# Stick-breaking attention: value products with the values stationary for pairs of heads, and their normalisation transposed

## The reference, cut to what matters

```python
def stick_breaking(q, k, v, qpos, kpos):
    z = jnp.einsum('bqhd,bkhd->bhqk', q, k).astype(jnp.float32) * (B_DIM ** -0.5)
    before = kpos[None, :] < qpos[:, None]
    log_keep = jnp.where(before, jax.nn.log_sigmoid(-z), 0.0)
    rev = lax.cumsum(log_keep, axis=3, reverse=True)
    after = jnp.concatenate([rev[..., 1:], jnp.zeros_like(rev[..., :1])], axis=-1)
    a = jnp.where(before, jnp.exp(jax.nn.log_sigmoid(z) + after), 0.0)
    return jnp.einsum('bhqk,bkhd->bqhd', a.astype(v.dtype), v)
...
ob = rms(ob) * p['g_sub_b']          # over the 64 columns of a head
o = jnp.concatenate([oa.reshape(b, t, A_WIDTH), ob.reshape(b, t, B_WIDTH)], axis=-1) @ p['w_out']
```

## Time and profile before

| | |
|---|---|
| median of 3 runs | 1125.89 us (1123.23 to 1126.4) |
| the profiled execution: its own time, its span | 1127.26 us, 1125.5 us |
| PE busy, share of the span | 1055.9 us, 94% |
| DVE, ACT, POOL busy | 397.8, 276.4, 293.9 us |
| attention B, first scores to first `w_out` product | 251.87 to 358.02 us |

### The profile page before, as it was taken

The page is one execution under the profiler, slowest core; times in us unless marked ns, Lnnn a source line. Parts: engine busy times, 40 slices in busy tenths (PEclk is TensorE's granted clock), DMA queues, the critical chain, the costliest instruction groups (busy, mean ns, idle before and its releaser), DMA issues.

```text
span 1125.5 us, 19301 instructions
## 1 busy us (share of the span) xinstructions
PE 1055.9 (94%) x6480; PEld 653.5 (58%) x6481; DVE 397.8 (35%) x956; ACT 276.4 (25%) x733; POOL 293.9 (26%) x494
## 2 busy tenths in 40 slices
PE   4999999999998999999999999999999999999792
PEld 1777755555765447666666555656565666665440
DVE  3633301655754227722222212222222222222157
ACT  3200013666653005011111111111111111111231
POOL 1000002003521000523434333333434433434200
PEclk9999999999999999999999999999999999999986
DMA  8722245007840008489989999999999999998951
GB/s 339 280 75 75 75 168 182 1 1 272 293 151 1 1 0 330 176 333 415 346 332 415 414 416 413 415 414 409 379 367 359 413 413 414 409 402 330 316 204 65
DMA packets 80516, 304.31 MB, mean 270 GB/s; under 512 B 13478, under 2 KB 15592, under 8 KB 63064
## 3 DMA queue, kind: packets, MB, share of 16 engines
q1 hardware_dynamic: 63560, 268.26, 61.0%
q0 software_dynamic: 16256, 33.08, 7.8%
q10 hardware_dynamic: 656, 2.36, 0.5%
HBM read 290.26 MB, written 33.82 MB: 288 GB/s over the span
## 4 chain that ended last, share of the span: by engine, by line
PE 58%; DMA 4%; DVE 3%; issue 2%; POOL 1%; SPq 1%; ACT 1%; ACTq 0%; POOLq 0%; DVEq 0%
PE bank L1105 26%; PE bank L1112 15%; PE bank L1027 5%; PE bank L1098 3%; DMA arena<-in_w_down 2%; PE bank L1117 2%; PE bank L1156 1%; PE bank L713 1%; PE bank L714 1%; PE bank L1186 1%; POOL arena L566 1%; DMA arena<-y_rows 1%; PE bank L1033 1%; DVE arena L1962 1%; DMA y_rows<-arena 1%
## 5 line engine op out<-in xcount | busy, mean ns | idle before, releaser
L1105 PE MATMUL bank<-arena 128*64 128x256 f32 x2880 | 329.0, 379 | 11.3 <-issue 8.6
L1105 PEld LDWEIGHTS bank<-arena 128*64 128x64 f32 x2880 | 246.2, 137 | 116.8 <-issue 60.8
L1939 DVE COPY arena<-bank 128x512 f32<-128x512 f32 x90 | 62.2, 692 | 327.2 <-PE bank L1098 327.2
L1112 PE MATMUL bank<-arena 128*64 128x512 f32 x728 | 176.3, 601 | 1.5 <-DVE arena L1933 0.6
L1437 ACT COPY arena<-bank 128x128 f32<-128x128 f32 x90 | 23.9, 266 | 407.2 <-PE bank L1117 407.2
L581 POOL DMA_INDIRECT arena<-h_rows,arena x93 | 98.4, 1058 | 82.7 <-POOL arena L578 78.2
L589 POOL DMA_INDIRECT y_rows<-arena x91 | 93.4, 1026 | 85.7 <-POOL arena L586 81.1
L762 PE MATMUL bank<-arena 128*128 128x288 f32 x448 | 108.9, 406 | 0.3 <-DVE arena L1586 0.3
L1933 DVE COPY arena<-bank 128x512 f32<-128x512 f32 x91 | 62.9, 692 | 103.0 <-PE bank L1112 99.9
L762 PEld LDWEIGHTS bank<-arena 128*128 128x128 f32 x448 | 85.0, 190 | 24.5 <-issue 1.1
L1112 PEld LDWEIGHTS bank<-arena 128*64 128x64 f32 x728 | 52.1, 136 | 67.2 <-issue 66.4
(11 more groups left out here) (289 smaller groups left out, 1092.9 us busy)
## 6 DMA issues: line engine op xcount, KB each, us to landing
arena<-in_w_gate SPq DMA_DIRECT2D x64, 1024.0 KB, 12.5
arena<-in_w_up SPq DMA_DIRECT2D x64, 1024.0 KB, 15.9
arena<-in_w_down SPq DMA_DIRECT2D x64, 1024.0 KB, 14.9
arena<-in_w_ada SPq DMA_DIRECT2D x8, 2048.0 KB, 11.1
arena<-in_w_in SPq DMA_DIRECT2D x5, 2048.0 KB, 8.0
arena<-in_w_ada SPq DMA_DIRECT2D x8, 1024.0 KB, 17.4
arena<-y_rows SPq DMA_DIRECT2D x4, 2048.0 KB, 8.4
arena<-in_w_out SPq DMA_DIRECT2D x2, 2048.0 KB, 9.8
```

The lines of the kernel that those rows point to most:

```text
L1105: last = pe.matmul(bank[0][n * SLOT:n * SLOT + SLOT, 0:2 * P].rearrange("p (g f) -> p g f", f=P), HGT[:, k % 4, k // 4, :], w[:, :, n * P: ...
L1112: last = pe.matmul(bank[3][n * SLOT:n * SLOT + SLOT, :], AE[:, f, :], DN[j][:, f, 512 * n:512 * n + 512], start=(f == 0), stop=(f == 1))
L1939: dve.tensor_copy(hgt, bank[1][:, :]).then_inc(hgt_ready, 1)
```

## The change

For the prompt, `pair_values(p)` takes the place of two `b_values`. The values (64 columns) are stationary and the weights move, 512, 384, 256 and 128 columns. The even head goes to partitions 0 to 63 and the odd one to 64 to 127 of all of bank 7. The output so has channels on partitions and queries in columns, which is how `OT` needs it: ACT's `pair_out` copies it straight into `OT[:, 4 + p]`, and PE's chunks 4 to 7 of the turn are gone. The mean of squares of a head now runs over partitions: DVE squares into `SQ` (`pair_square`), PE multiplies by a block matrix `PAIR` of 1/64 (`pair_squares`, again into bank 7), ACT takes the logarithm with a bias (`pair_log`), then the exponential of -0.5 times it (`pair_root`), and DVE multiplies (`pair_norm`). `b_mean`, `b_rms` and `b_norm` remain for the sample alone.

The orders, where "2p" is the pair whose turn it is: PE has `pair_squares(p-2)` behind `b_scores(2p)` and `pair_values(p-1)` behind the `ada` products, nothing behind `b_sums(2p+1)`. ACT has `pair_log(p-2)` and `pair_out(p-1)` behind `b_log(2p+1)`, and `pair_root(p-2)` between `b_exp(2p)` and `b_exp(2p+1)`. DVE has `pair_norm(p-2)` and `pair_square(p-1)` at the end of the round.

```diff
@@ -156,6 +156,8 @@
         BR = at(take(NE), NE)
         SQ = at(a_keep + 1024, 512)
         GA = at(take(2), 2)
+        PAIR = at(take(P), P)
+        EPST = at(take(1), 1)
         SS = at(take(NT), NT)
@@ -262,6 +264,9 @@
         sa_done, sa_read, ea_done, wa_ready, wta_done, wta_evac, pva_done, oa_evac = map(
             sem, ("sa_done", "sa_read", "ea_done", "wa_ready", "wta_done", "wta_evac", "pva_done", "oa_evac"))
         z_half = sem("z_half")
+
+        pair_sq, pair_ms, pair_ln, pair_rs, pair_ready = ada_ld[0], ada_ld[1], ada_ld[6], ada_ld[7], in0_ld[0]
+        PAIR_BASE = 16
         abs_ready, fade_ready, ls_ready, z_done, lk_ready, p_done, eb_done, at_ready, pvb_done, ob_evac, lk_ln = map(
             sem, ("abs_ready", "fade_ready", "ls_ready", "z_done", "lk_ready", "p_done", "eb_done", "at_ready", "pvb_done", "ob_evac", "lk_ln"))
@@ -495,7 +500,7 @@
 
             def b_rms(h):
 
-                pool.wait_ge(osb_ready, h + 1)
+                pool.wait_ge(osb_ready, 1)
                 pool.tensor_tensor(b_stat(OR, h), b_stat(OS, h), b_stat(HALF, h), ALU.pow).then_inc(orb_ready, 1)
 
             def later_logs(h):
@@ -540,11 +545,6 @@
                 if p == 0:
                     pool.wait_ge(osa_ready, 1)
                     pool.tensor_tensor(OR[:, :, 0:HA], OS[:, :, 0:HA], HALF[:, :, 0:HA], ALU.pow).then_inc(ora_ready, 1)
-                else:
-                    b_rms(2 * p - 2)
-                    b_rms(2 * p - 1)
-            b_rms(HB - 2)
-            b_rms(HB - 1)
             masks(HB)
             b_rms(HB)
-            def turn_chunk(src, k):
+            def turn_chunk(src, k, step=1):
                 for t in range(4):
                     last = pe.transpose(bank[k % 4][:, t * P:t * P + P], src[:, t, k * P:k * P + P], IDENT)
-                last.then_inc(tr_done, 1)
-
-            def turn(src, r, half=None, sample=None, begun=0, only_prompt=False):
+                last.then_inc(tr_done, step)
+
+            def turn(src, r, begun=0, only_prompt=False):
 
 
 
                 for k in range(begun, KC):
-                    if k == 4 and half:
-                        pe.wait_ge(*half)
                     if k >= 4:
 
                         pe.wait_ge(tr_act if k % 2 else tr_dve, (4 if k % 2 else 5) * r + (k - 4) // 2 + 1)
                     turn_chunk(src, k)
                 if not only_prompt:
-                    turn_sample(src, sample)
+                    turn_sample(src)
 
             def turn_sample(src, sample=None, odd_apart=False):
@@ -960,21 +958,32 @@
                 return last
 
 
-            def b_values(h):
-                if h >= 1:
-                    pe.wait_ge(ob_evac, h)
+            def pair_values(p):
+
+                if p:
+                    pe.wait_ge(pair_ln, PAIR_BASE + p)
                 else:
                     pe.wait_ge(proj_dve, NT)
-                if h in (HB - 2, HB - 1):
+                if p == HB // 2 - 1:
                     unread(7)
-                pe.wait_ge(at_ready, 3 * h + 3 if h < HB else 3 * HB + 1)
-                if h < HB:
-                    for i in range(4):
-                        for j in range(i + 1):
-                            o = ZO[j] + (i - j) * P
-                            last = pe.matmul(bank[7][:, i * DB:i * DB + DB], AT[:, h % 2, o:o + P], V[:, j, 512 + h * DB:512 + h * DB + DB],
-                                             start=(j == 0), stop=(j == i))
-                else:
+                pe.wait_ge(at_ready, 6 * p + 6)
+                for j in range(4):
+                    for h in (2 * p, 2 * p + 1):
+                        o = h % 2 * DB
+                        last = pe.matmul(bank[7][o:o + DB, j * P:TP], V[:, j, 512 + h * DB:512 + h * DB + DB], AT[:, h % 2, ZO[j]:ZO[j] + ZW[j]],
+                                         start=(j == 0), stop=(j == 3), skip_group_check=True)
+                last.then_inc(pvb_done, 1)
+
+            def pair_squares(p):
+
+                pe.wait_ge(ob_evac, p + 1)
+                pe.wait_ge(pair_sq, PAIR_BASE + p + 1)
+                pe.matmul(bank[7][:, :], PAIR, SQ, start=True, stop=True).then_inc(pair_ms, 1)
+
+            def b_values(h):
+                pe.wait_ge(pair_ln, PAIR_BASE + HB // 2)
+                pe.wait_ge(at_ready, 3 * HB + 1)
+                if h == HB:
                     pe.wait_ge(eb_done, 3 * HB + 3)
                     for x in range(HB // 2):
                         for j in range(3):
@@ -989,30 +998,34 @@
 
             for p in range(HB // 2):
                 b_scores(2 * p)
-                if p:
-                    b_values(2 * p - 1)
-                else:
+                if p >= 2:
+                    pair_squares(p - 2)
+                if p == 0:
                     for k in range(KC):
                         value_b_step(4 * KC + k)
                 ada(ADA_FIRST + 2 * p, G_ADA + 2 * p)
                 ada(ADA_FIRST + 2 * p + 1, G_ADA + 2 * p + 1)
+                if p:
+                    pair_values(p - 1)
                 b_sums(2 * p)
                 b_sums(2 * p + 1)
-                if p < HB // 2 - 1:
-                    b_values(2 * p)
             b_scores(HB)
-            b_values(HB - 2)
+            pair_squares(HB // 2 - 2)
             ada_turn_later()
-            b_values(HB - 1)
+            pair_values(HB // 2 - 1)
             b_sums(HB)
+            pair_squares(HB // 2 - 1)
             pe.wait_ge(mod_ready, 12)
             on_rows(16, 0, 5, 6).then_inc(g1_mm, 1)
             b_values(HB)
 
             pe.wait_ge(eb_done, 3 * (HB + 1))
             pe.wait_ge(on_ready, NT)
-            turn(OA, 1, half=(on_ready, NT + HB), sample=(on_ready, NT + HB + 1))
+            for k in range(4):
+                turn_chunk(OA, k, 2)
+            turn_sample(OA, (on_ready, NT + 1))
             turned(1)
+            pe.wait_ge(pair_ready, PAIR_BASE + HB // 2)
             on_rows(16, 1, 7, 4).then_inc(g1_mm, 1)
             for n in range(2):
                 pe.wait_ge(ring_ld[(G_OUT + n) % 3], ring_count(G_OUT + n))
@@ -1212,15 +1225,15 @@
                 act.wait_ge(done, before)
                 act.activation(junk[0:r, :], X[0:r, t, :], ACT.Square, accum_out=SS[0:r, t:t + 1]).then_inc(done, 1)
 
-            def turned(r, dst, scale, shift, ks=range(1, KC, 2)):
+            def turned(r, dst, scale, shift, ks=range(1, KC, 2), step=1):
 
                 for k in ks:
@@ -1346,16 +1359,27 @@
                     r, o, w, b = b_part(h, s)
                     act.wait_ge(p_done, 3 * h + x + 1)
                     if h >= 2 and x == 0:
-                        act.wait_ge(pvb_done, h - 1)
+                        act.wait_ge(pvb_done, h // 2)
                     act.activation(AT[0:r, h % 2, o:o + w], b[0:r, 0:w], ACT.Exp).then_inc(eb_done, 1)
 
-            def b_out(h):
-                act.wait_ge(pvb_done, h + 1)
-                if h < HB:
-                    act.copy(OA[:, 0:4, 512 + h * DB:512 + h * DB + DB], bank[7][:, 0:4 * DB].rearrange("p (t d) -> p t d", d=DB)).then_inc(ob_evac, 1)
-                else:
-                    act.copy(OA[0:TS, 4, 512:768], bank[7][0:TS, 0:256])
-                    act.copy(OA[0:TS, 4, 768:D], bank[7][TS:P, 0:256]).then_inc(ob_evac, 1)
+            def pair_out(p):
+                act.wait_ge(pvb_done, p + 1)
+                act.copy(OT[:, 4 + p, 0:TP], bank[7][:, :]).then_inc(ob_evac, 1)
+
+            def pair_log(p):
+
+                act.wait_ge(pair_ms, PAIR_BASE + p + 1)
+                act.activation(SQ, bank[7][:, :], ACT.Ln, bias=EPST[:, 0:1]).then_inc(pair_ln, 1)
+
+            def pair_root(p):
+
+                act.wait_ge(pair_ln, PAIR_BASE + p + 1)
+                act.activation(SQ, SQ, ACT.Exp, scale=-0.5).then_inc(pair_rs, 1)
+
+            def b_out():
+                act.wait_ge(pvb_done, HB // 2 + 1)
+                act.copy(OA[0:TS, 4, 512:768], bank[7][0:TS, 0:256])
+                act.copy(OA[0:TS, 4, 768:D], bank[7][TS:P, 0:256]).then_inc(ob_evac, 1)
 
 
             for p in range(HB // 2):
@@ -1363,20 +1387,25 @@
                 b_fade(2 * p + 1)
                 b_log(2 * p)
                 b_log(2 * p + 1)
+                if p >= 2:
+                    pair_log(p - 2)
                 if p:
-                    b_out(2 * p - 1)
+                    pair_out(p - 1)
                 b_exp(2 * p)
+                if p >= 2:
+                    pair_root(p - 2)
                 b_exp(2 * p + 1)
-                if p < HB // 2 - 1:
-                    b_out(2 * p)
             b_fade(HB)
-            b_out(HB - 2)
             b_log(HB)
-            b_out(HB - 1)
+            pair_log(HB // 2 - 2)
+            pair_out(HB // 2 - 1)
             b_exp(HB)
-            b_out(HB)
-
-            turned(1, OT, lambda k: GA[:, k // 4:k // 4 + 1], None)
+            pair_root(HB // 2 - 2)
+            pair_log(HB // 2 - 1)
+            pair_root(HB // 2 - 1)
+            b_out()
+
```

(55 more changed lines are left out.)

2 lines of the change are left out of this document (added).

## The result

The changed kernel takes 1141.65 us (median of 4 runs, 1139.17 to 1144.87) against 1124.8 us (4 runs): the ratio is 1.0146, 95% interval 1.0130 to 1.0161. It is slower, as forecast, but by 16.8 us where 11.1 were forecast, and 0.65 us above the range. Measured a second time, in five runs beside eleven of the kernel before, it took 1140.02 us against 1126.19, ratio 1.0125 (1.0109 to 1.0140), 13.8 us. The profiled execution took 1139.17 us, the fastest of the first four; its span is 1137.4 us, 11.9 over that of before.

What follows compares the result with a forecast made beforehand. It took PE and the start of `w_out` after attention B to bound the kernel: +7.9 us of rounds and waits plus +3.2 of PE's clock made +11.1, from 1125.9 to 1137.0 us; range 1131.5 to 1141.

Steps and rivals of the forecast that it cites:

- The wait on bank 7: Rounds 2 and 3: PE stands 3.2 us ahead of `pair_values` until ACT's `pair_log` is done; rounds +2.5 and +3.9 us.
- T + 6.85 and T + 10.05: Round 2, T being the start of its scores: PE reaches `pair_values` at 6.85 us, ACT ends `pair_log` at 10.05.
- Round 0: First pair's round: `b_values(0)` no longer stands between the sums and the next scores, -1.4 us.
- Round 1: Second pair's round: sums start at T + 8.35 as before, round 16.3 us instead of 17.8, -1.5 us.
- No transfer is added or moved: Whole kernel: SP's and POOL's queues wait only on `ada_done` and `wo_done`, which move with PE; no cost counted.
- The ninth round's chain: Ninth round: PE stands 2.4 us for `pair_log(2)`, then 2.7 us for exponential, root, norm and square; +4.4 us.
- U + 39.1: Forecast start of `w_out`, U being the start of the ninth round's scores; U + 34.7 before.
- PE's clock: One drop to half rate for each wait of rounds 2 and 3, 1.6 us each: +3.2 us; bounds nothing to +6.4.
- Rival 2: The clock drops in the ninth round too: +12.7 to +14.3 us, 1139 to 1140; 12%.
- 1: Rival: waits are there, the clock holds in at least one of rounds 2 and 3: +7.9 to +9.5 us; 23%.
- 3: Rival: the halves of `pair_values` don't run together, 2.2 us more in each of four, +8.8: 1146 us; 5%.
- 4: Rival: not slower, `pair_log` is done when PE arrives: -0.9 us, 1125; 6%.
- 5: Rival: a wait costs less, or part of the delay is taken up behind `w_out`: +3.5 to +6 us; 9%.

Runs made afterwards that it cites:

- log_first: The changed kernel with `pair_log` moved ahead of the pair's own two logarithms on ACT: 1132.58 us, ratio 1.0056 to the kernel before.
- copy_root: The changed kernel with DVE copying the mean squares out of bank 7 and `pair_root(2)` ahead of the sample's exponentials on ACT: 1123.42 us, ratio 0.9982.
- fill_all: fill_ninth plus, in rounds 2 and 3, the mean-square product moved behind the `ada` products and done three times: 1134.41 us, ratio 1.0072.
- fill_ninth: The changed kernel with dense filler products on PE in four idle stretches of the ninth round and behind it, every wait kept: 1135.55 us, ratio 1.0081.
- root_first: The changed kernel with `pair_root(2)` moved ahead of the sample's exponentials on ACT: 1138.62 us, ratio 1.0111 to the kernel before.
- log_root: The changed kernel with `pair_log` ahead of the pair's own logarithms and `pair_root(2)` ahead of the sample's exponentials, no copy: 1129.55 us, ratio 1.0029.
- values_only: The changed kernel with stationary values for pairs kept but the normalisation of the prompt's heads in attention B left out: 1135.8 us, ratio 1.0093.
- copy_root_fill: copy_root with five dense filler products on PE in the two idle stretches behind the turned chunks: 1121.08 us, ratio 0.9956.

## Why the prediction was right in direction and wrong in size

**The wait on bank 7: right, in place, cause and size.** T + 6.85 and T + 10.05 were forecast for PE's arrival and ACT's logarithm; measured T + 7.06 (with the square at 1.06 instead of 0.88) and T + 10.03, with `pair_values` at T + 10.08. `log_first` and `copy_root` take the wait away in two ways, and the rounds follow.

**Round 0: right.** 17.46, and without the luck of the clock 18.9 before: 1.4 less. The tail of the exponential left PE idle 0.69 us.

**Round 1: wrong by 0.9.** The step that failed is "No transfer is added or moved". The scores start 3.0 us earlier than before (269.43 against 272.42) and `b_values` no longer stands behind them, so the first `ada` product starts 5.4 us earlier (271.79 against 277.16), and the second is due before its weights: 0.83 us of waiting on the transfer, 0.9 to 1.4 in the other profiles of the changed product.

**The ninth round's chain: right.** Waits of 3.15 and 2.81 where 2.4 and 2.7 were forecast, the first 0.7 longer, since the forecast's 9.7 us for the sample's scores had the old `unread` ahead of `b_values(6)` in it (they take 8.78); `fill_all` gives 39.2 us for the forecast's U + 39.1.

**PE's clock: this term was mis-sized, and mis-placed.** The step was "I take one drop for each of the two, at 1.6 us", for rounds 2 and 3, and nothing in the ninth. Measured: 5.5 us in the ninth round in both profiles of the changed kernel (44.65 - 39.16), 4.5 us by the medians (`fill_ninth`); in rounds 2 and 3 nothing in three profiles and 4.6 us in one (21.94 + 22.39 - 20.31 - 19.45, `root_first`). Rival 2 had named the ninth round's drops, but at 1.6 each and at 12%. The assumption that the longest idle stretch is the likeliest to bring a drop was the error. Around 3.0 us of idle time among `ada` products and scores of 256 to 512 columns the clock mostly held. In the ninth round, where PE had done 8.8 us of score products 64 columns wide with three of 512 between and the short products of `ada_turn_later`, it fell with 3.15 us of idle time, with 1.59 (`log_first`, `log_root`), and in `values_only` with none. It did not fall there in `copy_root` and `copy_root_fill`, which have no wait either and one product of 512 columns more than `values_only`. So the waits are not shown to be what brings the drop; `fill_ninth` shows what the drops cost. The price was low too: of the three stretches at half rate in the ninth round and over the start of `w_out` the first and the last run 6.8 us, and only the second 3.4.

With these put in, 7.9 + 0.9 + 5.5 + 0 to 4.6 = 14.3 to 18.9, and the two measurements gave 13.8 and 16.8, the first half a microsecond under the lower end, within its interval (12.3 to 15.8). The profiled execution's +11.9 agrees with the forecast of 11.1 by accident: it lacks the 1.7 us at the first scores that the profile of before has, and 1.3 us behind `w_out`.

**The pages named in the prediction.** The Trainium skill, "TensorE: Matmul & The Clock Gate", section "HAM oscillation — how this bites in real kernels", says that waits between bursts of matmuls can put the clock down again each time. The traces agree in the ninth round of the changed kernel, where three stretches at half rate stand in or behind its four waits, and only in part in rounds 2 and 3 (two falls at eight waits of 3.02); the fall of `values_only` has no wait ahead of it. The Trainium skill, "ScalarE: Activation LUTs", section "Table sets: the hidden batching unit", says that one set holds exponential and logarithm. That does not save the loads here: the changed kernel has a load of 1.28 at each switch, and 12 in all by the stage's timeline.

**The rivals.** 1 had the waits with the clock held in rounds 2 and 3, and both profiles of the changed kernel show just that; its price of 7.9 to 9.5 was too low, since it too had nothing in the ninth round. 2 named the ninth round, as told above. 3 (halves in turn) fell: 2.37 us. 4 (no wait) fell: 3.02. 5 fell: from `w_out` on the changed kernel takes 766.4 us, the kernel before 767.7, and of the others all but `values_only` 765.3 to 768.7.

**What stays open.** In which executions the clock falls in rounds 2 and 3, and what brings the fall in the ninth round: no run changes only what PE does ahead of it, or only the wait. The falls in rounds 2 and 3 may well be what moves medians of five or six runs by 1 to 2 us, but `fill_all` did not narrow the spread, and the times alone could not show `root_first`'s gain.

## What to carry to other kernels

A bank that gets a second use is held until its last reader is done, and if that reader stands in a batch on another engine (here: to share a table load), the batch's end becomes the writer's start. Look for the engine with a gap at that point and let it carry the tile out: 0.68 us on DVE took away two 3 us waits and a third that, with the clock, cost three times its length (`log_root` against `copy_root`). When PE work is removed from a stage, price the stretch with the clock too, and there look at what PE does around the wait, not at the wait's length alone. An ablation that changes data ahead of a routing decision is read from its stage, since the total may carry something else (here 12 us).

## What the runs showed of the hardware that was not expected

- Eleven more products made the kernel 4.5 us faster (`fill_ninth`).
- A wait of 1.59 us came with 6.8 us at 1.2 GHz, the clock falling 0.4 us into the wait in `log_first` and some 1.1 us in `log_root`; waits of 3.02 us among dense products had none behind them in six of eight cases. In `values_only` the clock fell with PE busy 10.55 of the 10.73 us before.
- The first scores of attention B, with the same 1.2 us of idle time ahead in every profile, took 2.43 us in some executions and 3.9 to 4.1 in others (the kernel before, `fill_ninth`, `values_only`, `copy_root`, `copy_root_fill`): the same instructions at the same place meet either clock.
